# Products that nobody reads in TensorE's four waits around the opening norm and the first block's result norm

## The reference

```python
shift, scl, gate = jnp.split(jax.nn.silu(c) @ w_ada + b_ada, 3, axis=-1)
h = rmsnorm(x, g_pre) * (1.0 + scl[:, None]) + shift[:, None]
ys = (short_conv_mixer(h, ...), nsa_mixer(h, ...), gmlp_mixer(h, ...))
...                       # merged: the three results, gated
out = rmsnorm(merged @ w_out, g_post)
return x + gate[:, None] * out
```

## Time and profile before

| | us |
|---|---|
| median of 3 runs | 2949.67 (2949.61 to 2949.86) |
| the profiled execution's own time | 2950.07 |
| its span, first to last instruction | 2948.3 |
| TensorE busy | 2829.5 (96%) |
| mean granted TensorE clock | 0.983 |

### The profile page before, as it was taken

How to read it: one execution, slowest core, us unless ns; L and a number is a source line. 1 busy time by engine, 2 the same in 40 slices (tenths; PEclk the granted TensorE clock), 3 DMA queues, 4 the chain that set the end, 5 groups by cost and what they waited for, 6 DMA issues and landing times. The chain is left out here.

```text
span 2948.3 us, 39997 instructions
## 1 busy us (share of the span) xinstructions
PE 2829.5 (96%) x16029; PEld 2310.9 (78%) x16029; DVE 1397.6 (47%) x2505; ACT 1137.0 (39%) x2060; POOL 1221.8 (41%) x586
## 2 busy tenths in 40 slices
PE   6999999999999989999999999999999899999998
PEld 4865568888988877777788999988787667888887
DVE  6336650342043362774554556532587553565620
ACT  4357762222244333443455422222343445522221
POOL 5432224454444532222214545554445423555553
PEclk9999999999999998999999999999999999999999
DMA  7410003223322211112324323233222223422232
GB/s 267 145 57 16 15 30 100 97 96 99 111 98 93 93 59 62 44 41 102 112 76 144 126 86 99 89 106 102 88 100 72 77 75 130 139 93 93 101 104 89
DMA packets 84088, 274.71 MB, mean 93 GB/s; under 512 B 9727, under 2 KB 9983, under 8 KB 83776
## 3 DMA queue, kind: packets, MB, share of 16 engines
q1 hardware_dynamic: 82568, 271.32, 27.6%
q10 hardware_dynamic: 1336, 0.83, 0.1%
HBM read 257.36 MB, written 17.90 MB: 93 GB/s over the span
## 5 line engine op out<-in xcount | busy, mean ns | idle before, releaser
L135 POOL TENSOR_TENSOR weights_lo<-weights_raw,weights_hi 128x1024 fp32r<-128x1024 f32 x413 | 1002.4, 2429 | 1344.5 <-ACT weights_hi L127 1344.4
L127 ACT ACTIVATE weights_hi<-weights_raw 128x1024 fp32r<-128x1024 f32 x413 | 435.3, 1058 | 1044.7 <-PE acc L548 436.5
L546 PE MATMUL acc<-h_hi,weights_hi 128*128 128x512 f32 (+1 forms) x1096 | 437.0, 399 | 22.2 <-POOL h_lo L1441 6.5
L547 PE MATMUL acc<-h_lo,weights_hi 128*128 128x512 f32 (+1 forms) x1096 | 424.4, 387 | 0.0
L548 PE MATMUL acc<-h_hi,weights_lo 128*128 128x512 f32 (+1 forms) x1096 | 424.3, 387 | 0.0
L546 PEld LDWEIGHTS acc<-h_hi,weights_hi 128*128 128x128 f32 x1096 | 208.5, 190 | 77.5 <-issue 31.6
L548 PEld LDWEIGHTS acc<-h_hi,weights_lo 128*128 128x128 f32 x1096 | 208.5, 190 | 42.0
L547 PEld LDWEIGHTS acc<-h_lo,weights_hi 128*128 128x128 f32 x1096 | 208.8, 191 | 36.5 <-issue 0.2
L546 PE MATMUL acc<-h,weights_hi 128*128 128x258 f32 (+2 forms) x592 | 182.9, 309 | 7.3 <-ACT gate_tiles L2652 4.0
L547 PE MATMUL acc<-h,weights_hi 128*128 128x258 f32 (+2 forms) x592 | 170.5, 288 | 0.0
L548 PE MATMUL acc<-h,weights_lo 128*128 128x258 f32 (+2 forms) x592 | 170.3, 288 | 0.0
(11 more groups left out here) (474 smaller groups left out, 6356.9 us busy)
## 6 DMA issues: line engine op xcount, KB each, us to landing
weights_raw<-in_stream SPq DMA_DIRECT2D x413, 512.0 KB, 3.3
weight_ring<-in_w_ada SPq DMA_DIRECT2D x24, 512.5 KB, 8.3
gates<-gate_tiles SPq DMA_DIRECT2D x24, 258.0 KB, 4.1
gate<-gates SPq DMA_DIRECT2D x8, 774.0 KB, 5.3
held<-gates SPq DMA_DIRECT2D x8, 768.0 KB, 6.2
gates<-gate_tiles SPq DMA_DIRECT2D x23, 256.0 KB, 4.0
bias_copies<-bias_rows SPq DMA_DIRECT2D x1, 3068.0 KB
table<-bias_copies SPq DMA_DIRECT2D x1, 2560.0 KB, 10.2
```

Source lines behind the costliest of these rows:

```text
L127: act.activation(self.hi[:, at % CUT, :], self.raw[:, at % RAW, :], ACT.Copy).then_inc(self.hi_done, 1)
L135: pool.tensor_tensor(self.lo[:, at % CUT, :], self.raw[:, at % RAW, :], self.hi[:, at % CUT, :].bitcast(F32), ALU.subtract).then_inc(self. ...
L546: pe.matmul(out, left[0], right[0], start=start, stop=False)
L547: pe.matmul(out, left[0], right[1], start=False, stop=False)
```

## The change

A new function issues n products of the identity (128 x 128) by 512 columns of a constant, plain f32, into a bank of its own, `unread`, which nothing reads. It is called at four places of TensorE's program: 6 products before the wait for `inverted` in the opening and 7 after its spreading products, 4 and 5 at the same places of the first block's result norm. No semaphore is added, and no other call of `Norm` gets a bank.

```diff
+def stay_busy(pe, k, acc, n):
+    for _ in range(n):
+        pe.matmul(acc[:, :], k.ident, k.causal[:, 0:512], start=True, stop=True)
@@ Norm.pe
+        if self.unread is not None:
+            stay_busy(pe, self.k, self.unread, 4)
         pe.wait_ge(self.loaded, 16)
         pe.wait_ge(self.inverted, 1)
...
         last.then_inc(self.spread, 1)
+        if self.unread is not None:
+            stay_busy(pe, self.k, self.unread, 5)
         yield
@@ Opening
+        self.unread = psum("unread", [P, 512])
@@ Opening.pe
+        stay_busy(pe, self.k, self.unread, 6)
         yield
         yield
         pe.wait_ge(self.rows_loaded, 16)
...
         last.then_inc(self.spread, 1)
+        stay_busy(pe, self.k, self.unread, 7)
         yield
@@ first_block
-                norm = Norm(..., total=scale[:, :])
+                norm = Norm(..., total=scale[:, :],
+                            unread=psum("unread", [P, 512]))
```

More of the change, by code:

```diff
@@ L936, with __init__ @@
 class Norm(Lane):
-    def __init__(self, sem, sbuf, k, A, source, T, n, w, ready, sums, wide, scale, cut=None, held=None, total=None, behind=False):
+    def __init__(self, sem, sbuf, k, A, source, T, n, w, ready, sums, wide, scale, cut=None, held=None, total=None, behind=False, unread=None):
         self.k, self.A, self.source, self.T, self.n, self.w, self.ready, self.behind = k, A, source, T, n, w, ready, behind
-        self.sums, self.wide, self.scale, self.cut = sums, wide, scale, cut
+        self.sums, self.wide, self.scale, self.cut, self.unread = sums, wide, scale, cut, unread
         self.loaded, self.squared, self.summed, self.mean_done = sem("loaded"), sem("squared"), sem("summed"), sem("mean_done")
@@ L2120, in first_block @@
                 led_of = Led(lambda t: k.vec[:, gain + t:gain + t + 1], raw, N2, W2, LED2, lead, [1.5, 1.5, 5, 5], [])
-                norm = Norm(sem, sbuf, k, A, lambda t: merged[:, t, :], S, 1, S, projected, sums, wide[:, 0:1, :], scale[:, :], total=scale[:, :])
+                norm = Norm(sem, sbuf, k, A, lambda t: merged[:, t, :], S, 1, S, projected, sums, wide[:, 0:1, :], scale[:, :], total=scale[:, :],
+                            unread=psum("unread", [P, 512]))
                 added = Residual(sem, lambda t: merged[:, t, :], lambda t: k.ada[:, 2 * KT + t:2 * KT + t + 1], scale[:, :],
```

## The result

| | us |
|---|---|
| after, median of 12 runs | 2954.91 (2947.74 to 2957.20) |
| before, median of 12 runs beside it | 2949.51 (2946.53 to 2950.80) |
| ratio | 1.0018 [1.001, 1.0026] |
| profiled execution of after, its span | 2951.83, 2950.1 |
| its mean granted clock | 0.988 (before 0.983) |

The change costs 5.4 us. That is 0.18%, just inside the bound that the prediction set for "no difference", but clear of its interval, and 3.6 us above the top of the range. The clock was granted more than before and the time is longer all the same.

A forecast was written before the change was run, and what follows sets the result against it. TensorE, busy 2829.5 of 2948.3 us, was taken to bound the kernel. The terms 0.01 + 0 - 0.07 = -0.06 us took 2949.67 to a forecast of 2949.6 us (chance 0.70), 8 in 10 range 2948.4 to 2951.3.

The forecast's parts named there:

- no difference: Whole kernel: about 0.2% (5.9 us) is what a measurement can tell from no change; chance of landing within it 0.95.
- the top of the range: Whole kernel's time: 2951.3 us, upper end of the 8 in 10 range that starts at 2948.4.
- The clock: Granted clock 1.00 from 29 to 43 and at 1050 to 1057, with the fall at 43.3 expected again.
- A (no fall): Opening: the clock does not fall at 43.3; at most 0.54 us won, time 2949.1; chance 0.10.
- D (the products don't hold the clock): Opening and result norm: half speed stays despite the added products, +3.8 and +4.3 us, time 2957.8; chance 0.03.
- The length of a product: Each added product at the upper clock: two records of 0.43 us, 0.86 in all, bounds 0.82 and 0.88.
- rival B: Added products: weight loads are not hidden, 0.38 us a product at worst, +5.7, time 2955.3 at worst; chance 0.07.
- The first two places: Opening, 6 products before the spread and 7 after: cost 0.01 and 0 us; opening's bounds -0.54 and +0.13.
- The last two: Result norm, 4 products before the spread and 5 after: spread 0.68 us late, then TensorE 0.07 earlier; sum -0.07.
- rival C: After the result norm: VectorE becomes the bound and the whole +0.68 shift stands, time 2950.3; chance 0.09.
- The sum: All four places: 0.01 + 0 - 0.07 = -0.06 us; 18.9 us of added work nearly all in waits and regained time.

## Why the prediction was wrong, step by step

- **The clock** came as forecast: 1.00 from 29 to 41 and from 1050 to 1052, the fall at 43.3 again (43.7), and the wait for `h_lo` tile 2. Rivals A (no fall) and D (the products don't hold the clock) are out.
- **The length of a product** was close: the timeline gives 5.42 us for 12 records that end with one of 0.6, so 0.437 a record, 0.874 a product, against 0.86 with 0.82 to 0.88. Weight loads are hidden, so rival B is out, though its times (2952 to 2955.3) hold the one measured; that is chance.
- **The first two places**: besides 6 x 0.014 the step missed about 0.09 us at each change between products of different operands, and the sums ended 0.20 later before any change. The spread came at 31.30, not 30.83; VectorE did not find it ready but waited 0.49. The opening is +0.55, not +0.01 (bound +0.13). The first projection product at 38.10 was forecast at 37.8.
- **The last two**: the spread came 1.73 later, at 1050.43; 0.76 of that came in from ahead, so 0.97 was its own, against 0.68, and the next sums at 1056.00 in place of 1054.65. TensorE sets the pace there, so rival C is out, and the place costs +0.5, not -0.07. The opening and the norm are mis-sized by about 1 us together.
- **The sum is the step that failed.** "Added work is 22 products, 18.9 us of TensorE's time; nearly all of it lies in waits and in time won back from the lower clock": the working counted the products' time, and no rival counted their 88 instructions. So the term that it put at nothing, without a reason, is what 88 more instructions do to the loads of TensorE's program. The kernels with the same instructions and no work cost +5.3 and +5.0; filling to a whole load takes back 3.7 on average. The mis-sized places, +0.55 and +0.5 by the profile, fit the +1.8 of the changed kernel with whole loads, but its interval holds zero, so that part is argued and not shown.

What stays open. Only one collision, the store at 1570, is seen to its end, and it explains 0.8 to 1.5 us of about 3.7. One of two later stores of `gates` is waited for longer as well (3.5 to 4.2 against 1.7 to 2.0) in every kernel with loads moved behind 1570 and in no other: the one near 2340 in the three kernels with 36 to 56 more instructions, the one near 2415 in the four with 88. But no step of TensorE goes with it. Near 2235, in the pair products of the third block, 5 of the 8 profiles with loads moved there have TensorE 4 to 5.6 us later behind it. Their half-speed stretch begins at about 2236 by the times of before, where TensorE is the bound; in the 13 other profiles it begins at 2226 to 2229, and none of the 10 without moved loads has the step. If 5 of 8 executions pay some 5 us there, that is about 3 us on average, which is of the size of the missing part; this is an estimate from eight single executions and not shown. The tiny-product kernel has it (PE, PEld, DVE, ACT, POOL, SP, clock), its filled partner has its half speed earlier:

```profile
2239.00:2242.00 3.00, 3.00 (x20) 2.61 (x19) 2.25 (x4) 0.00 (x0) 0.52 (x1) 0.56 0.53 208
2242.00:2246.00 4.00, 4.00 (x11) 3.13 (x10) 1.60 (x6) 0.00 (x0) 0.00 (x0) 0.50 0.00 0
```

```profile
2228.00:2231.00 3.00, 1.73 (x8) 1.76 (x9) 2.96 (x6) 0.63 (x1) 1.28 (x1) 0.60 0.00 0
2231.00:2234.00 3.00, 3.00 (x15) 2.90 (x15) 2.80 (x7) 1.79 (x3) 0.60 (x1) 0.50 0.02 5
```

In the second TensorE waits for part of that stretch (1.73 of 3.00 busy), so little is lost; in the first it is busy throughout. This goes together with the loads; why the clock falls later I have not shown, and the profiled executions are single ones (that of after does not have the step and ended only 1.8 later than before's, though its median is 5.4 higher). How the cost divides over the two halves of the move is open for the same reason.

## What to carry to other kernels

An added instruction can cost more than its time: it moves every later load of the engine's own program, and a load that meets a transfer which somebody waits for is paid far away. Whether a given move costs or gives depends on what it meets: here part loads of 56 to 88 instructions cost 2.7 to 4.8 us against whole ones. So judge an edit of the instruction count against a control with as many instructions and no work, or fill it to a whole load (here 256 instructions, 64 products of 4 x 8, 3.35 us in the last kernel, in a wait that exists anyway). Size filling work to end before the wait does, change of operands included: the same idea, four products shorter at each norm and filled to a load, went from +5.4 to -3.9 us.

## What the runs showed of the hardware

- A 16.4 KB load of TensorE's program is one packet on one DMA engine, for 0.9 to 1.9 us in the loads around 1570. When the last 8 of a store's 128 packets began only behind it, the 258 KB store landed in 3.9 to 4.5 us where it took 2.1 to 2.3 (8 profiles against 10).
- A plain f32 product of 128 x 128 by 512 columns is two records 0.437 us apart, a product of 4 columns of weights by 8 two records 0.025 to 0.027 apart. The weight loads of the former lie beside the records and add nothing. Changing from one kind of product to the next cost about 0.09 us.
- 22 tiny products at the four places did not keep the clock up: the half-speed stretch at the result norm was 6.8 or 10.2 us with them (3 profiles) and 6.8 or 10.2 with nothing there (9 profiles). It was absent in all 6 profiles with full products there, 1.98 us of them or more ahead of the spread.
- Single executions of one kernel before spread from 2947.0 to 2955.2 us over 21 runs on one chip, where the three shown lie within 0.25. How far they lay apart told nothing of how far the next would.
